# A decoder trunk step on one core: the embedding's products ahead of the gate's in each unit of the gate stage

## What is computed

```
h = x + jnp.concatenate([ya, yb], axis=-1) @ w_out
gate = jax.nn.sigmoid(rms_norm(h, g_ple) @ w_pg)
return h + (p @ w_ple) * gate
```

## Time and profile before

| | |
|---|---|
| median of 3 runs | 2392.67 us (2391.92 to 2398.38) |
| profiled execution | 2398.78 us, span 2397.0 us |
| PE busy | 2341.2 us (98%) |
| DVE, ACT, POOL busy | 830.6, 637.2, 768.4 us |
| DMA | 294.25 MB, mean 123 GB/s |

### The profile page before, as it was taken

One profiled execution on the slowest core, in us unless ns is written; L12 is line 12 of the kernel. 1 busy time (PEld: TensorE's weight loads), 2 busy tenths in 40 slices (PEclk: granted clock), 3 DMA queues, 4 the chain that ended last, 5 costly groups with the idle time before them and its releaser, 6 DMA issues.

```text
span 2397.0 us, 40204 instructions
## 1 busy us (share of the span) xinstructions
PE 2341.2 (98%) x16009; PEld 2229.2 (93%) x16009; DVE 830.6 (35%) x2232; ACT 637.2 (27%) x1881; POOL 768.4 (32%) x783
## 2 busy tenths in 40 slices
PE   5999999999999999999999999999999999999997
PEld 4999999999999999888888999999999999999996
DVE  7013333233333404444555434242212262211253
ACT  5122222222222312223444310210000132222444
POOL 2332222222222132221222223333333334454564
PEclk8999999999999999999999999999999999999998
DMA  5233233333333325444454454533323344333685
GB/s 191 65 113 98 78 104 96 80 110 96 82 106 90 88 78 151 134 134 142 144 164 143 129 172 126 178 114 94 98 86 96 122 146 129 106 112 103 176 246 190
DMA packets 383795, 294.25 MB, mean 123 GB/s; under 512 B 53807, under 2 KB 347927, under 8 KB 382319
## 3 DMA queue, kind: packets, MB, share of 16 engines
q1 hardware_dynamic: 342261, 249.43, 35.6%
q10 hardware_dynamic: 41347, 42.25, 5.3%
HBM read 225.38 MB, written 66.22 MB: 122 GB/s over the span
## 4 chain that ended last, share of the span: by engine, by line
PE 90%; DVE 4%; DMA 3%; ACT 1%; POOL 1%; SPq 0%; issue 0%; DVEq 0%; ACTq 0%; POOLq 0%
PE psum L1074 26%; PE psum L1076 25%; PE psum L1075 25%; PE psum L855 3%; PE psum L877 2%; PE psum L888 2%; PE psum L962 1%; PE psum L949 1%; PE psum L932 1%; DMA y_in<-yt_scratch 1%; DVE x_n L1590 1%; PE psum L914 1%; DVE act_lo L1581 1%; PE psum L1214 1%; PE psum L1128 1%; PE psum L979 1%
## 5 line engine op out<-in xcount | busy, mean ns | idle before, releaser
L1074 PE MATMUL psum<-act_hi,w_hi 128*128 128x344 f32 x4032 | 1313.3, 326 | 2.6 <-DVE act_lo L1859 0.9
L1076 PE MATMUL psum<-act_hi,w_lo 128*128 128x344 f32 x4032 | 1288.4, 320 | 0.0
L1075 PE MATMUL psum<-act_lo,w_hi 128*128 128x344 f32 x4032 | 1287.2, 319 | 0.0
L1074 PEld LDWEIGHTS psum<-act_hi,w_hi 128*128 128x128 f32 x4032 | 759.5, 188 | 13.4 <-issue 9.8
L1075 PEld LDWEIGHTS psum<-act_lo,w_hi 128*128 128x128 f32 x4032 | 758.9, 188 | 0.2
L1076 PEld LDWEIGHTS psum<-act_hi,w_lo 128*128 128x128 f32 x4032 | 758.6, 188 | 0.0
L809 POOL CAST w_hi<-w_raw 128x512 fp32r<-128x512 f32 (+1 forms) x352 | 225.1, 639 | 1519.7 <-PE psum L1076 1356.8
L811 POOL TENSOR_TENSOR w_lo<-w_raw,w_hi 128x512 fp32r<-128x512 f32 (+1 forms) x390 | 504.5, 1294 | 63.5 <-ACT w_hi L1529 35.1
L1673 DVE COPY prob_t<-psum 128x512 f32<-128x512 f32 (+1 forms) x56 | 35.5, 635 | 448.8 <-PE psum L888 448.8
L1943 DVE TENSOR_TENSOR t_gate<-psum,acc 128x344 f32<-128x344 f32 x48 | 24.8, 516 | 255.9 <-PE psum L1076 255.9
L1878 DVE TENSOR_TENSOR h_row<-psum,h_row 128x344 f32<-128x344 f32 x48 | 22.9, 516 | 243.9 <-PE psum L1076 230.8
(11 more groups left out here) (212 smaller groups left out, 1982.9 us busy)
## 6 DMA issues: line engine op xcount, KB each, us to landing
w_raw<-in_w_in SPq DMA_DIRECT2D x208, 256.0 KB, 3.0
w_raw<-in_w_pg SPq DMA_DIRECT2D x94, 256.0 KB, 3.0
w_raw<-in_w_out SPq DMA_DIRECT2D x64, 256.0 KB, 2.7
z_scratch<-stage ACTq DMA_DIRECT2D x72, 172.0 KB, 1.9
h_scratch<-h_row ACTq DMA_DIRECT2D x16, 516.0 KB, 2.7
x_in<-in_x_prompt SPq DMA_DIRECT2D x8, 1024.0 KB, 5.0
zq<-z_scratch SPq DMA_DIRECT2D x32, 256.0 KB, 4.3
o_scratch<-ot SPq DMA_DIRECT2D x32, 256.0 KB, 3.4
```

The lines of the kernel that those rows point to most:

```text
L1074: pe.matmul(psum[:, bank, 0:T3], hi_w, hi_a[:, k, rows], start=(k == 0), stop=False, skip_group_check=True)
L1075: pe.matmul(psum[:, bank, 0:T3], hi_w, lo_a[:, k, rows], start=False, stop=False, skip_group_check=True)
L1076: return pe.matmul(psum[:, bank, 0:T3], lo_w, hi_a[:, k, rows], start=False, stop=stop, skip_group_check=True)
```

## The change

In every unit from the fourth on (u = 3), PE begins with the embedding's 6 products and ends with the gate's 48. The list of groups follows: from tile 1 on, the embedding's group comes before the tile's four gate groups, in both passes. With it, the last gate group of a tile becomes the one whose use is told by `u_produced`, and the embedding's group is told by `w_used`. ACT rounds all five groups of a tile in one go, at the place where it rounded the four gate groups. Unit 0 to 2, the number of groups, the places in SP's queue at which the other transfers stand, and the tail are as before.

```diff
-    out += [(what, n, k, WG if what == "gate" else 2) for n in range(KT) for what, ks in (("gate", parts), ("ple", (0,))) for k in ks]
-    out += [(what, n, k, WG if what == "gate2" else 2) for n in range(1, KT) for what, ks in (("gate2", parts), ("ple2", (0,))) for k in ks]
+    first = (("gate", parts), ("ple", (0,)))
+    later = (("ple", (0,)), ("gate", parts))
+    second = (("ple2", (0,)), ("gate2", parts))
+    out += [(what, n, k, WG if what == "gate" else 2) for n in range(KT) for what, ks in (later if n else first) for k in ks]
+    out += [(what, n, k, WG if what == "gate2" else 2) for n in range(1, KT) for what, ks in second for k in ks]
...
-SECOND_GROUP = GROUP["gate2", 1, 0]
+SECOND_GROUP = GROUP["ple2", 1, 0]
...
-        elif what == "ple":
-            out.append(("u_produced", UNIT[i, 1 if i else 2] + 1))
-        elif what == "ple2":
+        elif what == "ple" and i == 0:
+            out.append(("u_produced", UNIT[i, 2] + 1))
+        elif what == "gate" and i and k + n == KT:
+            out.append(("u_produced", UNIT[i, 1] + 1))
+        elif what == "gate2" and k + n == KT:
             out.append(("u_produced", UNIT[i, 2] + 1))
...
-                mm.then_inc(sem("u_produced"), 1)
+                if n == 0:
+                    mm.then_inc(sem("u_produced"), 1)
+                elif t:
+                    mm.then_inc(sem("w_used"), 1)
...
+                embedding(u)
                 pe.wait_ge(sem("g_scaled"), u - 2)
...
-                    if t and k % WG == WG - 1:
+                    if k == KT - 1:
+                        mm.then_inc(sem("u_produced"), 1)
+                    elif t and k % WG == WG - 1:
                         mm.then_inc(sem("w_used"), 1)
                     if u == 3 * KT - 1 and k == KT // 2:
                         y_turn(u - 1)
-                embedding(u)
...
-                if 1 <= u - SECOND + 2 < KT:
-                    round_weights(u - SECOND + 2, 4)
...
-                    for part in range(4):
+                    for part in range(5):
                         round_weights(u - SECOND + 3, part)
```

More of the change, by code:

```diff
@@ L764, in _ @@
                 for part in range(5):
-                    weights(GROUP["gate", n, 0] + part + 7)
+                    weights(GROUP["gate", 0, 0] + 5 * n + part + 7)
                 if n == 2:
@@ L773, in _ @@
                 for part in range(5):
-                    weights(GROUP["gate2", n, 0] + part + 9)
+                    weights(SECOND_GROUP + 5 * (n - 1) + part + 9)
                 if n == 2:
@@ L1521, in round_weights @@
             def round_weights(tile, part):
-                g = GROUP["gate2", tile, 0] + part
+                g = SECOND_GROUP + 5 * (tile - 1) + part
                 n = GROUPS[g][3]
```

## The result

The changed kernel takes 2399.84 us (median of 13 runs, 2397.44 to 2402.94), the kernel before 2394.93 us (13 runs beside it, 2391.92 to 2398.38). The ratio is 1.0022, 95% interval 1.0015 to 1.003, so +3.6 to +7.2 us, middle 5.3. The forecast was +4.1 us and "same within 0.3%" with 0.75; its time of 2396.8 us counted from a median of 3 runs that lay 2.3 us lower. The profiled execution took 2398.35 us (span 2396.5), less than that of before (2398.78): it was a low one of its kernel, 1.5 us under the median, and that of before a high one, 3.9 us over. That is no contradiction: its unit 0 ended 3.9 us earlier (1970.12 against 1974.00), after stages that are the same in both, and it gave 3.7 of that back in the second pass. So the two profiles are compared by stretches of the second pass, not by their spans, and even so their 3.7 us are less than the 5.3 us of 13 runs each.

The account below looks back on a forecast made before the run. PE, busy 98% of the span, was taken to bound the kernel; 0.1 + 0.5 + 2.5 + 1.0 = +4.1 us, carried to the median of 2392.67, gave 2396.8 us, range 2390 to 2405.

Parts of the forecast that it names:

- The count of work: Whole kernel: no product, rounding, split or byte is added or removed, and the last unit's end costs 0.
- the first pass: First pass over the weights: a group serves two units and PE never waited there, so 0.
- unit 3: Its embedding, now first, waits for DVE's `t_y` of unit 0; cost about 0.1 us.
- ACT's order: Late fifth group now ahead of ACT's next sigmoid, `h_in` load and y copy; cost 0.
- Deadline of the fifth group: Second pass: the tile's fifth weight group must land 0.5 us sooner, paid once at the latest landing: 0.5 us.
- The loop: Second pass, chain of load, rounding, split, next issue: 0.5 us more a period, 2.5 us up to the worst landing, 1.0 behind.
- The queue is always full: Rival on the DMA queue: only deadline and unit 3 count, +0.6 us or nothing, 2393.0 us; chance 0.22.
- Latency bounds: Rival: each period grows its full 1.3 us, PE stands in nearly every unit from 2270 us, +13.1 us; chance 0.20.
- the worst landing: Latest arrival of a fifth group, near 2320 us, with five periods before and five behind; wait forecast 3 to 7 us.
- The late group no longer hurts: Rival: ACT's 20.8 us wait vanishes, the gate's last quarter arrives in time, 5.6 us come back, 2387.1 us; chance 0.09.
- The signs in the profile: What the new profile would show if right: unit lengths, ACT's and PE's waits, and spacing of the fifth group's roundings.
- the 5.6 us lost in the profile of before: Second pass: 120.44 us for 13 units against 114.8 undisturbed; all that a better order could win back, 0.23%.

Follow-up runs that it names:

- e2: New order in the first pass only (units 3 to 32), second pass as in the kernel before; ratio 0.9999 to the kernel before.
- e3: Changed kernel, but ACT rounds the fifth group again behind the next unit's sigmoid; ratio 1.0033 to the kernel before.
- e4: Changed kernel, but SP issues each megabyte of rows one weight group later, behind the gate's last group; ratio 0.9991 to the kernel before.
- e6: Changed kernel with six raw weight places instead of four in the second pass; ratio 0.9984 to the kernel before, median 2391.51 us.
- e8: Changed kernel with the final norm's rows loaded, scaled and stored behind all weights; ratio 1.0069 to the kernel before, 2411.20 us.
- e1: New order in the second pass only (units 33 to 47), first pass as in the kernel before; ratio 1.0028 to the kernel before.
- e11: Kernel before, but SP issues each megabyte of rows one weight group earlier, ahead of the fourth gate group; ratio 1.0029 to the kernel before.
- e12: Changed kernel, but each megabyte of rows is issued one weight group earlier, ahead of the gate's third group; ratio 1.0029 to the kernel before.
- e5: Kernel before with six raw weight places instead of four in the second pass; ratio 0.9987 to the kernel before, median 2391.85 us.
- e9: Kernel before, but ACT and POOL work on a full 128x512 area for the second pass's embedding group, no bytes added; ratio 1.0014.

## Why the prediction was right, step by step

**The count of work, the first pass, unit 3.** Right: e2 is at 0.9999, and unit 3 costs 0.18 us (0.1 said).

**ACT's order: 0.** Right in that undoing it regains nothing (e3).

**Deadline of the fifth group.** The 2.1 us from rounding to product measured 2.09. Its 0.5 us can't be seen by itself: by e4, e6 and e8 PE's order costs nothing when the gate's last group doesn't stand behind the rows, or isn't late there.

**The loop.** Right as a mechanism, and of the rivals none came whole. *The queue is always full* is refuted by e6, with a share of 0.95 and no loss. The rule of the Trainium skill that it drew on ("DMA: Bandwidth & Descriptors", "Queues, rings and completion order": a queue's descriptors are consumed in ring order) isn't touched by this: in the profiles of both kernels the late group is the one behind the rows. But when SP issues a load is a matter of the kernel's own places, and here that was what counted. *Latency bounds* stated its own point, landings more than about 9.6 us apart in the stretch of stores: they were 9.92 apart, past it, and PE stood again in four of the last five whole units. So behind the worst landing this rival was the better description; its sum of +13.1 us didn't come, for ahead of that landing the periods hardly grew. *The late group no longer hurts* fell with PE's 5.8 us of waits.

**The sizes.** Here the terms of the sum were off, in opposite ways.

Ahead of the worst landing I took 5 x 0.5 = 2.5 us for the loop. The five periods grew from 10.15 to 10.30 us, 0.8 in all, and e2 and e1 give the same two numbers within 0.04 (10.15 and 10.34). My reading, which no run tests by itself: there more transfers were waiting in the queue (two megabytes at once in the worst period), as the prediction said of the load of 2311.78 and then didn't count. What the stretch costs in time is less sure: it hangs on the clock too, for which the sum has no term. With the deadline's 0.5 I had 3.0 us; the change's 66.33 us are 0.8 more than the 65.55 of before, but 2.7 more than the 63.63 of e2 (2256.52 to 2320.15), which has the second pass of before and kept its full clock.

Behind the worst landing I took 1.0; the profiles show 2.9, and e1 against e2 3.0 (58.02 and 54.99 us). There a period grew by 1.21 us and not by 0.5, close to the upper bound of 1.3. This is the term that was plainly too small.

So the total of the second pass, 4.0 us forecast, is near the 3.7 of the two profiles partly because errors cancel, and that is luck. Against e2's profile the change lost 5.5 us, and the 13 runs say 5.3. What the 0.5 us a period had mixed up, by this reading: the lateness and the bytes are mostly absorbed where the queue has a backlog, and nearly fully paid where it has none, instead of half everywhere.

**The signs in the profile.** Four came: units of 8.81 us up to 2270, ACT's long waits on `in_w_pg`, PE's waits before `act_hi` in the last quarter, periods of 10 to 11 us ahead of the worst landing. Two didn't: the worst wait was 2.54 us and not 3 to 7, and the periods behind it were 9.92 us, above the 9 to 9.5. And the 6.1 us by which the profile of before lay above its median, carried over to the change, had no match: the change's profile lay 1.5 us below its own.

**The chain itself** was described one link short. I read that the megabyte's issue waits for the split of the former fifth group, but not that five groups over four places make this so for any position; e11 and e12 were expected faster for that reason.

**What was to be gained.** I took the 5.6 us lost in the profile of before as the price. e5, with nothing lost, is only 2.8 us below in the medians (ratio 0.9987, so 1 to 5 us). That profile was a bad one: it took 2398.78 us, and e2's lost 3.8.

## What to carry to other kernels

When loads run ahead over a ring of places and a large transfer stands at one point of the queue, find the group behind it and follow its chain: landing, preparation, release of the place, next issue. With a tile of five groups and four places the transfer's own issue hangs on that group, so put the smallest and fastest-prepared group there, or add places (six were enough here) so that the chain is longer than the tile. A DMA share of 0.85 is no sign of a full queue: look at whether it rises when the chain is opened.

## What the runs showed of the hardware that I had not expected

PE's clock fell after its longest wait in the profiles of both kernels. In the profile of the change:

```profile
2317.00:2320.00 3.00, 2.42 (x12) 2.43 (x13) 2.97 (x4) 2.09 (x9) 2.33 (x2) 0.80 0.46 136
2320.00:2323.00 3.00, 3.00 (x15) 2.93 (x14) 1.19 (x2) 0.63 (x1) 3.00 (x3) 0.63 1.01 357
2323.00:2327.00 4.00, 4.00 (x28) 4.00 (x27) 0.42 (x1) 1.46 (x7) 2.08 (x3) 1.00 0.90 241
```

The wait that ended at 2317.57 was 2.54 us; the mean granted clock is then 0.80 and 0.63 of full speed, a mix of the 2.4 and 1.2 GHz levels, and full again from 2323 on. The units from 2307.76 to 2330.77 took 12.93 + 10.08 = 23.0 us for 17.6 undisturbed: 5.4 us lost for waits of 0.38 and 2.54 us in these two units. So a wait of 2.5 us cost about twice its length, in the kernel before as well (2.42 and 0.16 us of waits, 5.0 us lost from 2311.33 to 2333.98). In e9 it followed one wait of 1.80 us: the clock was 0.50 from 2320 to 2322 us, and two units lost 3.8 us. In e2 waits of 1.69 and 0.93 us, which ended 2.5 us apart, left it at 1.00, and two units lost 3.1 us for 2.6 of waits. The four waits that followed in the change, of 0.43 to 1.11 us and 2.9 us together, left no such mark: the windows from 2330 to 2381 us show a clock of 1.00, and the units lost 3.4 us (57.82 behind 2320.69, less 10.08 for the first, four of 8.81 and 9.14 for the last).
